# Modulation product in fp32 in four column groups, in a DiT block stack on one core

## The reference

```python
def modulate(x, shift, scale):
    return rms_norm(x) * (1.0 + scale) + shift
def adaln(cond, w, b):
    return jnp.split(jax.nn.silu(cond) @ w + b, 6, axis=-1)
```

## Time and profile before

| | |
|---|---|
| three runs | 3149.65, 3150.62, 3152.99 us |
| the profiled execution: span | 3154.0 us, granted clock 0.965 |
| its distance to the median of the runs | 3.4 us |
| busy: TensorE, weight loads, VectorE, ScalarE, GpSimd | 94%, 76%, 57%, 36%, 10% |
| DMA | 409.33 MB, mean 130 GB/s |
| slabs of `ada_w` | 24 of 2048 KB, median 7.8 us from issue to landing |

### The profile page before, as it was taken

How to read it: one execution, slowest core, us unless ns; L and a number is a source line. 1 busy time by engine, 2 the same in 40 slices (tenths; PEclk the granted TensorE clock), 3 DMA queues, 4 the chain that set the end, 5 groups by cost and what they waited for, 6 DMA issues and landing times. The chain is left out here.

```text
span 3154.0 us, 55883 instructions
## 1 busy us (share of the span) xinstructions
PE 2964.0 (94%) x24726; PEld 2386.1 (76%) x24726; DVE 1796.9 (57%) x2769; ACT 1140.6 (36%) x1779; POOL 300.5 (10%) x390
## 2 busy tenths in 40 slices
PE   7999998899998988898989999999899999999999
PEld 3775535899985468888949989876799897455898
DVE  3348566756554067778736555467555554465553
ACT  2236402434331234344223343444543433144432
POOL 2222011000000013323210000000000000200000
PEclk9999999999999999999989999999999999999999
DMA  7323544355543010000035545543355554423353
GB/s 263 104 107 107 187 149 146 117 188 192 191 172 120 27 28 3 3 3 3 32 132 177 190 161 179 180 156 134 100 168 181 165 178 174 139 75 132 109 187 134
DMA packets 258170, 409.33 MB, mean 130 GB/s; under 512 B 18647, under 2 KB 111208, under 8 KB 257800
## 3 DMA queue, kind: packets, MB, share of 16 engines
q1 hardware_dynamic: 253832, 392.50, 36.2%
q0 software_dynamic: 4096, 13.25, 1.5%
HBM read 400.68 MB, written 2.95 MB: 128 GB/s over the span
## 5 line engine op out<-in xcount | busy, mean ns | idle before, releaser
L353 DVE TENSOR_TENSOR ring_parts<-ring,arena_parts 128x2048 fp32r<-128x2048 f32 x270 | 598.4, 2256 | 285.7 <-ACT arena_parts L346 283.2
L346 ACT CAST arena_parts<-ring 128x2048 fp32r<-128x2048 f32 x270 | 495.4, 1885 | 517.1 <-PE psum L2822 229.5
L2822 PE MATMUL psum<-arena_parts 128*128 128x256 f32 x2816 | 514.6, 286 | 3.1 <-DVE arena_parts L578 2.1
L2822 PEld LDWEIGHTS psum<-arena_parts 128*128 128x128 f32 x2816 | 445.3, 195 | 4.2 <-DVE arena_parts L578 3.0
L2822 PE MATMUL psum<-arena_parts,ring_parts 128*128 128x256 f32 x1408 | 401.7, 285 | 0.0
L390 PE MATMUL psum<-arena_parts 128*128 128x512 f32 x1024 | 327.0, 393 | 2.0 <-DVE arena_parts L578 2.0
L2822 PEld LDWEIGHTS psum<-arena_parts,ring_parts 128*128 128x128 f32 x1408 | 274.0, 195 | 0.0
L1855 PE MATMUL psum<-arena_parts 128*128 128x512 f32 x768 | 236.6, 389 | 0.0
L390 PEld LDWEIGHTS psum<-arena_parts 128*128 128x128 f32 x1024 | 193.8, 190 | 43.0 <-DVE arena_parts L578 2.7
L390 PE MATMUL psum<-ring_parts,arena_parts 128*128 128x512 f32 x560 | 219.5, 392 | 0.0
L1840 PE MATMUL psum<-arena_parts 128*128 128x256 f32 x896 | 163.3, 285 | 4.2 <-DVE ring_parts L353 4.0
(11 more groups left out here) (498 smaller groups left out, 5888.1 us busy)
## 6 DMA issues: line engine op xcount, KB each, us to landing
ring<-in_mlp_w SPq DMA_DIRECT2D x48, 2048.0 KB, 8.2
ring<-in_ada_w SPq DMA_DIRECT2D x24, 2048.0 KB, 7.8
ring<-in_ffn_pre_w_gu SPq DMA_DIRECT2D x44, 1024.0 KB, 6.6
ring<-in_ffn_post_w_gu SPq DMA_DIRECT2D x44, 1024.0 KB, 7.1
ring<-in_ffn_pre_w_down SPq DMA_DIRECT2D x8, 2048.0 KB, 7.8
ring<-in_xmem_wkv SPq DMA_DIRECT2D x8, 2048.0 KB, 8.0
ring<-in_ffn_post_w_down SPq DMA_DIRECT2D x8, 2048.0 KB, 7.7
ring<-in_ab_w_in SPq DMA_DIRECT2D x7, 2048.0 KB, 7.7
```

Source lines behind the costliest of these rows:

```text
L346: nc.scalar.copy(high_view(name)[:, k, :], raw_view(name)[:, k, :]).then_inc(*up(act, ("high", name, h)))
L353: nc.vector.tensor_tensor(low_view(name)[:, k, :], raw_view(name)[:, k, :], high_view(name).bitcast(F32)[:, k, :], ALU.subtract)\
L2822: ins = nc.tensor.matmul(psum[:, b, 256 * j:256 * j + 256], s[:, k, at:at + P], x_parts[q][:, k, :], start=(k == 0 and i == 0), stop=(k == ...
```

## The change

All three parts are now done in fp32 and in the same way. The stationary operand is always 32 columns wide, so a matmul fills one of TensorE's four column groups, and its result goes to the 32 PSUM partitions of that group. Block `k` of the contraction goes to group `k % 4`: a piece of the generator is now four matmuls, for the four groups, on half a slab. The bias goes to group 0, the other groups begin with `start=True`. So the bank holds four partial sums; ScalarE copies all 128 partitions (to `ada_groups`, a scratch tile), and the turning matmul uses `fold` (1 where `p % 32 == f`) in place of the identity, which adds the four. Where rows are stored too (parts 1 and 2), one more matmul with `fold` adds them (`ada_sum_pe`). The split of part 1 is gone: its casts, its subtractions, `conditions_dve`, its 128 matmuls. The pieces are placed anew: in the attentions one after every second unit, in the decay 1 and 5, in the mLSTM one after the scores and one after every second step. Part 2's rows are stored after `merge_pool` rather than ahead of it, since the sum is done after the merge.

```diff
     blocks = {
         "ident": p == f,
-        "pairsum": (p % 32 // 4 == np.arange(32)[None, :] // 2) & (p % 2 == np.arange(32)[None, :] % 2),
+        "fold": p % 32 == np.arange(32)[None, :],
...
         def ada_matmuls(pe, part):
...
-            nc.tensor.matmul(rows, ident[at, at], adab[at, :], start=True, stop=False)
+            nc.tensor.matmul(psum[0:32, b, :], ident[at, base:base + 32], adab[at, :], start=True, stop=False)
             for i in range(ns):
                 name = (f"ada{layer}", n0 + i, 0)
-                for k in range(KT):
+                for k0 in range(0, KT, 4):
                     stage(pe, "ada")
                     s = slab(pe, name)
-                    ins = nc.tensor.matmul(rows, csil[:, k, 22 - 2 * i:22 - 2 * i + 2 * ns], s[:, k, :],
-                                           start=False, stop=(i == ns - 1 and k == KT - 1))
-                    if k == KT - 1:
+                    for g in range(4):
+                        k = k0 + g
+                        ins = nc.tensor.matmul(psum[32 * g:32 * g + 32, b, :], csil[:, k, 22 - 2 * i:54 - 2 * i], s[:, k, :],
+                                               start=(i == 0 and k0 == 0 and g > 0), stop=(i == ns - 1 and k0 > 0))
+                    if k0:
                         event = ("ada", "full", part) if i == ns - 1 else None
...
-            nc.scalar.copy(adab[base:base + rows, :], psum[0:rows, ADA_BANK[part], :])\
-                .then_inc(*up(act, ("read", ("ada", part))))
+            nc.scalar.copy(ada_groups, psum[:, ADA_BANK[part], :]).then_inc(*up(act, ("read", ("ada", part))))
             also(("ada", "rows", part), ("read", ("ada", part)))
 
         def ada_turn_pe(pe, part, b):
+
             stage(pe, "ada")
             layer, n0, ns, base = ADA_PARTS[part]
-            at = slice(base, base + 2 * ns)
             pe.wait_ge(*when(("ada", "rows", part)))
             pe.wait_ge(*bank(b, ("mod", part)))
             for j in range(4):
-                ins = nc.tensor.transpose(psum[:, b, 2 * ns * j:2 * ns * j + 2 * ns], adab[at, P * j:P * j + P], ident[at, at])
+                ins = nc.tensor.matmul(psum[:, b, 2 * ns * j:2 * ns * j + 2 * ns], ada_groups[:, P * j:P * j + P],
+                                       cst("fold")[:, 0:2 * ns], start=True, stop=True)
             ins.then_inc(*up(pe, ("mod", "turned", part)))
 
-        def ada_turn_sum_pe(pe, b, b2):
+        def ada_sum_pe(pe, part, b):
 
             stage(pe, "ada")
-            layer, n0, ns, base = ADA_PARTS[1]
-            at = slice(base, base + 4 * ns)
-            pair = cst("pairsum")[at, 0:2 * ns]
-            pe.wait_ge(*when(("ada", "rows", 1)))
-            pe.wait_ge(*bank(b, ("mod", 1)))
-            for j in range(4):
-                ins = nc.tensor.matmul(psum[:, b, 2 * ns * j:2 * ns * j + 2 * ns], adab[at, P * j:P * j + P], pair,
-                                       start=True, stop=True)
-            ins.then_inc(*up(pe, ("mod", "turned", 1)))
-            pe.wait_ge(*bank(b2, "sum"))
-            nc.tensor.matmul(psum[0:2 * ns, b2, :], pair, adab[at, :], start=True, stop=True).then_inc(*up(pe, "sum full"))
-
-        def ada_sum_act(act, b2):
+            layer, n0, ns, base = ADA_PARTS[part]
+            pe.wait_ge(*bank(b, ("sum", part)))
+            nc.tensor.matmul(psum[0:2 * ns, b, :], cst("fold")[:, 0:2 * ns], ada_groups, start=True, stop=True)\
+                .then_inc(*up(pe, ("sum full", part)))
+
+        def ada_sum_act(act, part, b):
             stage(act, "ada")
-            layer, n0, ns, base = ADA_PARTS[1]
-            act.wait_ge(*when("sum full"))
-            nc.scalar.copy(adab[base:base + 2 * ns, :], psum[0:2 * ns, b2, :]).then_inc(*up(act, ("read", "sum")))
+            layer, n0, ns, base = ADA_PARTS[part]
+            act.wait_ge(*when(("sum full", part)))
+            nc.scalar.copy(adab[base:base + 2 * ns, :], psum[0:2 * ns, b, :]).then_inc(*up(act, ("read", ("sum", part))))
 
         def ada_turn_dve(dve, part, b):
             stage(dve, "ada")
...
@@ -1202,10 +1131,10 @@
 
             for step, i in unit_tick(len(units), scores, None, turn, values):
                 step(i)
-                if queue is not None and step is values:
+                if queue is not None and step is values and i % every == every - 1:
                     fill(pe, queue, each)
 
-        def att_dve(dve, key, units, scale, probs=True, after_first=(), mem_after={}, rows=None, split=None):
...
@@ -1550,7 +1472,7 @@
                     ins = nc.tensor.matmul(psum[:, 1, P * t:P * t + P], kbT[:, h, P * t:P * t + P],
                                            qbT[:, h, P * t:P * t + P], start=True, stop=True)
                 ins.then_inc(*up(pe, ("ml", "S full", h)))
-                fill(pe, queue, 2)
+                fill(pe, queue, 1)
                 for z in range(2):
                     pe.wait_ge(*bank(2 + z, ("ml", "M", h, z)))
                     nc.tensor.matmul(psum[:, 2 + z, :], sel[0:4, h, :], gm[0:4, z, :], start=True, stop=True).then_inc(*up(pe, ("ml", "M full", h, z)))
                         nc.tensor.matmul(psum[:, b, 129:258], qbT[:, h, s], mlC[:, z, :], start=True, stop=True).then_inc(*up(pe, ("ml", "P full", i, z)))
-                        fill(pe, queue, 2)
+                        if z:
+                            fill(pe, queue, 1)
 
         def ml_act(act):
...
-            ada = [ada_matmuls(pe, 0), ada_split_matmuls(pe), ada_matmuls(pe, 2)]
-            fill(pe, ada[0], 16)
+            ada = [ada_matmuls(pe, part) for part in range(3)]
+            fill(pe, ada[0], 4)
             first_turn_pe(pe, "L0a")
-            fill(pe, ada[0], 8)
+            fill(pe, ada[0], 2)
             first_turn_pe(pe, "C0a")
-            fill(pe, ada[0], 8)
+            fill(pe, ada[0], 2)
             fill(pe, ada[0], 1)
             ada_turn_pe(pe, 0, 3)
             ab_in_pe(pe)
             qk_norm_pe(pe)
-            att_pe(pe, "na", na, [("read", ("qkT", i)) for i in range(8)], ada[1], 1)
-            att_pe(pe, "cx", cxa, (), ada[1], 1)
+            att_pe(pe, "na", na, [("read", ("qkT", i)) for i in range(8)], ada[1], 1, 2)
+            att_pe(pe, "cx", cxa, (), ada[1], 1, 2)
             fill(pe, ada[1], 1)
-            fill(pe, ada[2], 4)
-            ada_turn_sum_pe(pe, 2, 3)
-            fill(pe, ada[2], 20)
+            fill(pe, ada[2], 1)
+            ada_turn_pe(pe, 1, 2)
+            ada_sum_pe(pe, 1, 3)
+            fill(pe, ada[2], 5)
             decay_pe(pe)
             mlT_pe(pe)
...
-            att_dve(dve, "na", na, 0.125, after_first=["bias ready"], split=lambda i: range(i, i + 1) if i < 3 else (3, 4) if i == 3 else range(i + 1, i + 2))
-            att_dve(dve, "cx", cxa, 0.125, split=lambda i: range(i + 17, min(i + 18, 32)))
+            att_dve(dve, "na", na, 0.125, after_first=["bias ready"])
+            att_dve(dve, "cx", cxa, 0.125)
             decay_dve(dve)
             decay_out_dve(dve)
...
             ml_pool(pool)
+            merge_pool(pool)
             ada_store_pool(pool, 2)
-            merge_pool(pool)
```

More of the change, by code:

```diff
@@ L950, in ada_store_pool @@
             layer, n0, ns, base = ADA_PARTS[part]
-            pool.wait_ge(*when(("read", "sum") if part == 1 else ("ada", "rows", part)))
+            pool.wait_ge(*when(("read", ("sum", part))))
             for v in range(2):
@@ L1167, in unit_tick, with att_pe @@
                         yield step, i - j
[L1169 removed]
+        def att_pe(pe, key, units, needs=(), queue=None, each=0, every=1):
             stage(pe, "att")
```

91 lines of the change are left out of this document (12 added, 79 removed).

## The result

The changed kernel takes 3100.3 us (median of four runs, 3097.6 to 3100.8), the kernel before, in the same comparison, 3150.84: a ratio of 0.9835, 95% interval 0.9821 to 0.9849. The changed kernel's profiled execution spans 3098.4 us. That is 55.6 us less than the span of the kernel before, where the medians differ by 50.5. The table does that. (A profile's span is also 1.8 us shorter than the time of the same execution, 3098.4 beside 3100.23.) Each number is the time between two instructions' starts; e11 is a second profile of the changed kernel.

What follows compares the result with a forecast made beforehand. TensorE, busy 94% of the span, was taken as the bound. Terms -7.4 - 19.6 + 2 - 26.6 + 1 = -50.6 took 3154.0 to 3103.4; 3.4 lower for the median gave 3100 us, range 3089 to 3126.

Steps and rivals of the forecast that it cites:

- Start: Kernel start, to the modulation columns on VectorE: slabs set the pace instead of TensorE, columns at 45.9 us, -7.4 us.
- projection: Stage between the start and the attentions' first scores: forecast unchanged, 0 us.
- decay: Between attentions and mLSTM: no gain from its six pieces, TensorE idles and restarts at half clock, +2 us (0 to +4).
- mLSTM: From the first head to the merge: VectorE's own work becomes the bound, 93.3 us plus 2 when cold, -26.6 us.
- what lies behind: Everything after the merge: moved forward unchanged and TensorE bound, 0 us.
- attentions: Both attentions: 36.2 us of split matmuls leave TensorE, 16 pieces at 1.1 us are added, -19.6 us in all.
- merge: After the mLSTM: one added fp32 summing matmul on the path, +1 us; later gates stay hidden.
- Price of a piece: TensorE time of four fp32 matmuls on half a slab: 1.1 us if four column groups run side by side.
- rows 9 and 10: Trace rows of 64x64 fp32 tiles on opposite corners: two run side by side and start out of program order.
- Rival (c): Half clock or a hidden TensorE chain in mLSTM and start, two us more a head: 3110 us, chance 0.15.
- (a): Column groups overlap only in pairs or weight loads show, 1.93 us a piece: about 3118 us, chance 0.22.
- (b): Column groups do not overlap on TensorE, 3.65 us a piece: about 3179 us, slower, chance 0.08.

Runs made afterwards that it cites:

- e11: The changed kernel, unchanged, profiled once more: 3100.3 us (3097.7 to 3109.5).
- e1: The changed kernel with all of its fp32 matmuls in column group 0 instead of four groups: 3180.9 us, ratio to the kernel before 1.0093.
- e2: The changed kernel with two column groups (block k to group k % 2) instead of four: 3119.6 us.
- e4: The changed kernel with part 2's pieces from its fourth slab on cut from 512 to 64 columns: 3102.55 us.
- e5: The changed kernel with part 2's turning and summing matmuls and their copies moved ahead of the merge: 3098.2 us, ratio to the kernel before 0.9839.
- e3: The kernel before, unchanged, profiled once more: 3149.66 us, profile span 3147.9.
- e6: The changed kernel with 8 of part 1's 16 pieces moved from the attentions to ahead of the decay, its turning after softplus: 3121.1 us.
- e7: The changed kernel with both moves: part 2's turning and sum ahead of the merge, 8 attention pieces ahead of the decay: 3090.3 us, ratio 0.9832.
- e10: The kernel with 8 attention pieces moved ahead of the decay, run once more unchanged: 3114.3 us.
- e9: The changed kernel with part 2's sum ahead of the merge, part 1 pieces in attention start gaps, 4 ahead of the decay: 3086.4 us, ratio 0.9794.

## Why the prediction was right

The time was forecast as 3100 and came as 3100.3. That is closer than its terms were. Start, projection, decay, mLSTM and what lies behind came within 1.4 us; the attentions gained 3.1 us more than forecast, the merge lost 2.2 more. In sum the stages gained 52.7 us between the means of the profiles, for 50.6 forecast. The last step held luck as well: the forecast of the span was 3103.4, and the two profiles span 3098.4 and 3098.1. The 3.4 us that were taken off for the median were not explained; about 4 us of the first profile of before are the collision in its projection, which the runs around the median need not have had.

- **Price of a piece (the prediction's unit).** Forecast 1.1, measured 1.00. The step that rows 9 and 10 were taken for (different groups run side by side, fp32 and its two passes included) is shown by e1, e2 and e4. The doubt that four groups share the rows, and so the loads would show, is gone: in e4 eight loads and eight matmuls take 0.25 us together. The Trainium skill, TensorE: Matmul & The Clock Gate, Part 3, states that weight loads run beside matmuls only in another row group; by that rule the forecast's estimate was 1.9 us, and the trace disagrees with it.
- **Start.** The slabs bound it, as worked out, to 0.1 us at the columns; e2 confirms it from the other side. The gain was 6.5 against the mean of two profiles of before, which itself moves by 1.6.
- **Attention.** Full units came out as forecast (3.70 + 2.67 = 6.37 for a pair, forecast 6.4; 4.15 in the second attention, forecast 4.2). The total is 98.4 or 93.2 us, by how long the clock stays at half at the start: a scatter of 5 us that the forecast didn't have, though it asked for the clock in the mLSTM.
- **Decay.** Forecast +2 for half clock, measured 0 against the mean (-0.8 and +0.7 against the two profiles). L1401 did take 0.8 us more, but behind it the kernel before was at half clock itself (0.50 from 372 to 381 us); the forecast costed the stage from L1479's 2.77 us, which began at the full clock, and the last transposes came out 0.85 us shorter (5.41 for 6.26).
- **mLSTM.** The sum over VectorE's own work gave 93.3 + 2 - 0.7; e4 shows that TensorE's pieces add 1 us. Rival (c), a clock or chain that costs 2 us more a head, is out. (It took the 3.29 us of the earlier trace rows for TensorE's idling; they are VectorE's wait for TensorE, which worked through 415 to 420 us and waited 2.72 us behind that.)
- **Merge.** The term that was mis-sized: "`ada_sum_pe(2)` adds one fp32 matmul of 512 columns ... on the path: **+1**". It measured +3.2. Two things were missed: the turning had become eight records of 128 rows for four of 24, and TensorE, after 3.15 us of waiting, did both at half clock, 1.83 us each, where the turning had taken 0.55. At the full clock, in e5, their rows last 0.97 and 1.04.
- **Projection.** Forecast unchanged, and so it is where no collision of VectorE with GpSimd falls: 171.7 in e3 and in the first profile after. The collision made 4.1 us more of it in the first profile of before and 1.3 in e11. The 11.17 us stood in that profile, beside 2.29 for its neighbours, and the working passed over it.
- **Rivals (a) and (b)** were costed at 3118 and 3179; the kernels that have their mechanism by construction, e2 and e1, measured 3119.6 and 3180.9. Both sums are some 3 us too low by their own terms: (a)'s leaves out the decay's +2 and the merge's +1, (b)'s the decay's +2 and the attention's +1.

The gates, the rings of slabs in the attentions and the mLSTM, and the MLP behind moved as forecast.

## What to carry to other kernels

A product with few output rows can have its contraction laid out over the column groups of TensorE: the streaming time goes down with their number, here 3.55, 1.85 and 1.00 us for the same eight records. What is left to pay is one matmul that sums the groups, and a turning that now reads all 128 rows, here 3.66 us at half clock on the path, which e5 could move into a gap. Such relief is worth its full size only where TensorE is the bound; where it feeds another engine's chain, add up that engine's own work, and take it as the floor. And when matmuls are freed to move, look for each of their followers on in-order engines: a copy that waits for a late slab held up exponentials behind it for 10 us.

## What the runs showed that was not expected

- The clock can stay at half though TensorE's records leave no gap: 37.5 us at 1.2 GHz with TensorE busy 7.00 of every 7 us (e6), in a stretch of small fp32 matmuls, while the same stretch ran at 2.4 GHz in e7 and in e10's profile. Where it fell at the same place with pieces in every second unit or in each, it came back after 3.4 to 10.2 us (before at 300.0 us, e2 and e3); at the start of the first attention it stayed at half for 10 to 27 us with such pieces too. The runs don't show what decides it.
- VectorE and GpSimd exclude each other for whole instructions: 2.29 us of subtraction took 8.95 to 11.17 us in nine of the thirteen profiles (before, e2, e4 to e7, e9 to e11), and each ended 2.15 us behind the end of GpSimd's operation. What it costs TensorE depends on the slack of the moment: 11.17, 10.44 and 9.12 us (before, e4, e2) made TensorE wait 2.2, 1.4 and not at all.
